# A mixture of experts in which the chosen tokens are fetched as rows from device memory and transposed, where products with selection matrices gathered them

## The reference, cut to what matters

```python
def expert_choice_ffn(h, w_router, w_gate, w_up, w_down):
    cap = CAPACITY_FACTOR * S // N_EXPERTS            # 64
    aff = jax.nn.softmax(h @ w_router, axis=-1)
    gates, idx = lax.top_k(aff.transpose(0, 2, 1), cap)
    xe = h[bidx, idx]                                  # the chosen tokens of each expert
    hg = jnp.einsum('becd,edf->becf', xe, w_gate)
    hu = jnp.einsum('becd,edf->becf', xe, w_up)
    y = jnp.einsum('becf,efd->becd', jax.nn.silu(hg) * hu, w_down)
    y = y * gates[..., None]
    return jnp.zeros_like(h).at[bidx, idx].add(y)
```

## Time and profile before

| what | value |
|---|---|
| runs | 2341.9 us median, 2340.33 to 2350.0 |
| the profiled execution | 2344.44 us, its span 2342.6 us |
| mean granted TensorE clock | 0.943 |
| PE busy, whole span | 2090.0 us (89%) |
| experts, from the first product of the first pair to the end of the span | 1862.65 to 2342.6 us |

### The profile page before, as it was taken

How to read it: one execution, slowest core, us unless ns; L and a number is a source line. 1 busy time by engine, 2 the same in 40 slices (tenths; PEclk the granted TensorE clock), 3 DMA queues, 4 the chain that set the end, 5 groups by cost and what they waited for, 6 DMA issues and landing times. The chain is left out here.

```text
span 2342.6 us, 31825 instructions
## 1 busy us (share of the span) xinstructions
PE 2090.0 (89%) x12889; PEld 1039.2 (44%) x12889; DVE 952.7 (41%) x1775; ACT 440.6 (19%) x877; POOL 238.7 (10%) x191
## 2 busy tenths in 40 slices
PE   7989898798998998979798977887889699999998
PEld 3553435543463343564443433455534444444442
DVE  1049678441116778743223542394321511111112
ACT  1010442121002144111222332321111200000000
POOL 0020410000011230000004540500000000000000
PEclk9989999899999999989899988898989799999999
DMA  4225110211214401120102101221045299999997
GB/s 157 68 106 197 46 39 30 70 40 55 98 49 171 162 10 39 36 101 27 57 18 72 37 27 41 68 73 38 11 148 209 120 392 420 421 420 420 421 420 305
DMA packets 63470, 330.03 MB, mean 141 GB/s; under 512 B 7280, under 2 KB 9840, under 8 KB 34928
## 3 DMA queue, kind: packets, MB, share of 16 engines
q1 hardware_dynamic: 63344, 328.27, 36.6%
HBM read 321.16 MB, written 6.29 MB: 140 GB/s over the span
## 5 line engine op out<-in xcount | busy, mean ns | idle before, releaser
L424 PE MATMUL ps<-store,side_ring 128*128 128x512 f32 x824 | 408.4, 625 | 17.2 <-DMA side_ring<-in_w_rwkv 6.6
L424 PEld LDWEIGHTS ps<-store,side_ring 128*128 128x128 f32 x824 | 146.2, 195 | 191.8 <-issue 168.6
L2561 PE MATMUL ps<-expert_ring,xe 128*64 128x512 f32 x1024 | 225.0, 597 | 3.6 <-DMA expert_ring<-in_w_expert 1.9
L337 PE MATMUL ps<-store,side_ring 128*128 128x512 f32 x384 | 169.5, 604 | 1.9 <-DVE store L303 1.9
L424 PE MATMUL ps<-store 128*128 128x512 f32 x256 | 122.9, 638 | 24.7 <-DMA store<-in_w_merge 24.1
L2561 PEld LDWEIGHTS ps<-expert_ring,xe 128*64 128x64 f32 x1024 | 73.3, 138 | 151.9 <-issue 149.8
L337 PEld LDWEIGHTS ps<-store,side_ring 128*128 128x128 f32 x384 | 74.5, 195 | 95.7 <-issue 93.4
L2589 PE MATMUL ps<-expert_ring,store 128*64 128x512 f32 x512 | 111.6, 594 | 1.4 <-DVE store L2646 1.4
L1641 PE MATMUL ps<-store,raw 128*128 128x512 f32 x256 | 110.7, 593 | 1.9 <-DVE store L303 1.9
L2618 ACT ACTIVATE store<-ps 128x1024 f32<-128x1024 f32 x16 | 16.4, 1024 | 420.5 <-PE ps L2561 420.5
L424 PEld LDWEIGHTS ps<-store 128*128 128x128 f32 x256 | 51.8, 205 | 93.4 <-issue 67.2
(11 more groups left out here) (430 smaller groups left out, 3148.7 us busy)
## 6 DMA issues: line engine op xcount, KB each, us to landing
expert_ring<-in_w_expert SPq DMA_DIRECT2D x192, 1024.0 KB, 16.8
mixed<-in_w_ada SPq DMA_DIRECT2D x24, 1024.0 KB, 4.8
side_ring<-in_w_attn SPq DMA_DIRECT2D x32, 512.0 KB, 3.7
side_ring<-in_w_rwkv SPq DMA_DIRECT2D x20, 512.0 KB, 4.2
raw<-in_ple_gate SPq DMA_DIRECT2D x16, 512.0 KB, 3.5
store<-in_w_merge SPq DMA_DIRECT2D x16, 512.0 KB, 3.9
side_ring<-in_w_conv SPq DMA_DIRECT2D x12, 512.0 KB, 3.3
gates_before<-gated SPq DMA_DIRECT2D x16, 256.0 KB, 2.0
```

What stands on the lines that cost most here:

```text
L337: last = nc.tensor.matmul(ps[:, u, :], ring[:, u, k, :], src[:, k, :], start=(k == 0), stop=(k == kt - 1))
L424: ins = self.nc.tensor.matmul(self.ps[:, self.banks[j % banks], :], self.ring[:, j % self.slots, k, :], self.src[:, k, :], start=(k == 0), ...
L2561: last = nc.tensor.matmul(ps[w, 2 * ep + half, :], xe[:, ep, k, :], ring[:, unit % SLOTS, k2, S * half:S * half + S], start=(k == 0), stop ...
```

## The change

The first pair is gathered as before. For the other seven pairs, the rows of `tokens` are written to a table in device memory (`token_rows`, 512 rows of 4 KB) by four transfers on SP's queue. 28 products with one column each (`number`) multiply `chosen` with a new constant, `token_number`, and give for each pair the list of 128 token numbers; DVE copies it to an integer tile. GpSimd then issues for each pair an indirect transfer that fetches 128 rows of 4 KB into one of two buffers, which lie over the first half of `tokens`. In the PE order of a pair, 4 transposes (`turn_rows`) stand in the place of each half of the gather. The loops over pairs now hold two pairs (`BODY = 2`), so that the two buffers have fixed addresses; SP's loop holds one turn of the ring. The order of the weights is the same.

```diff
+    parts["token_number"] = i[:, None] + P * np.arange(TT)[None, :]
...
-                with sp.Fori(0, PAIRS - 1) as r:
-                    for i in range(UNITS):
-                        j = i + SLOTS
-                        sp.wait_ge(used[i % SLOTS], r * TURNS + i // SLOTS + 1)
-                        sp.dma_start(ring[:, i % SLOTS], w_expert[r + j // UNITS, j % UNITS]).then_inc(landed[i % SLOTS], 16)
...
+                sp.wait_ge(h_copied, KT)
+                for t in range(TT):
+                    sp.dma_start(rows_out[t * P:(t + 1) * P, :], tokens[:, t, :]).then_inc(s["rows_out"], 16)
+                with sp.Fori(1, PAIRS * UNITS // SLOTS) as turn:
+                    for i in range(SLOTS):
+                        sp.wait_ge(used[i], turn)
+                        sp.dma_start(ring[:, i], w_expert[turn * SLOTS + i]).then_inc(landed[i], 16)
+                sp.wait_ge(s["rows_landed"], PAIRS - 1)
...
+                def number():
+
+                    for i in range(1, PAIRS):
+                        for t in range(TT):
+                            last = nc.tensor.matmul(ps[:, 3, i:i + 1], chosen[:, t, 2 * i:2 * i + 2, :].rearrange("p e c -> p (e c)"),
+                                                    M.c("token_number")[:, t:t + 1], start=(t == 0), stop=(t == TT - 1))
+                    last.then_inc(s["numbered"], 1)
+
+                def turn_rows(tiles, buf):
+
+                    for k in tiles:
+                        last = nc.tensor.transpose(ps[:, k // 4, (k % 4) * P:(k % 4 + 1) * P], rows[:, buf, k * P:(k + 1) * P],
+                                                   M.c("ident"))
+                        if k % 4 == 3:
+                            last.then_inc(s["gathered"], 1)
...
                         if not final:
-                            gather(range(4 * ep, 4 * ep + 4), lambda t: chosen[:, t, bass.ds(r * 2 + 2, 2), :].rearrange("p e c -> p (e c)"))
+                            if ep == 0:
+                                pe.wait_ge(s["rows_landed"], r + 1)
+                            turn_rows(range(4 * ep, 4 * ep + 4), (1 + half_body) % 2)
...
                 gather(range(KT), lambda t: chosen[:, t, 0:2, :].rearrange("p e c -> p (e c)"), 6)
                 pe.wait_ge(s["all_chosen"], TT)
-                pair(0, first=True)
-                with pe.Fori(1, PAIRS - 1) as r:
-                    pair(r)
-                pair(PAIRS - 1, final=True)
+                number()
+                pair(-1, 1, first=True)
+                with pe.Fori(0, PAIRS // BODY - 1) as b:
+                    for half_body in range(BODY):
+                        pair(b, half_body)
+                pair(PAIRS // BODY - 1, 0, final=True)
...
+            @block.gpsimd
+            def _(pool):
+                pool.wait_ge(s["numbers_ready"], 1)
+                pool.wait_ge(s["rows_out"], 16 * TT)
+                pool.wait_ge(s["gathered"], 2)
+                for i in range(1, PAIRS):
+                    if i >= 3:
+                        pool.wait_ge(s["gathered"], 2 * (i - 1))
+                    nc.gpsimd.indirect_dma_start(rows[:, (i - 1) % 2, :], None, rows_out,
+                                                 bass.IndirectOffsetOnAxis(ap=numbers[:, i:i + 1], axis=0)).then_inc(row[i - 1], 16)
+                    pool.wait_ge(row[i - 1], 16)
+                    pool.sem_inc(s["rows_landed"], 1)
...
                     nc.vector.tensor_copy(xe[:, :, 4 * b:4 * b + 4, :], gathered(6 + b)).then_inc(s["x_ready"], 1)
+                dve.wait_ge(s["numbered"], 1)
+                nc.vector.tensor_copy(numbers[:, 1:PAIRS], ps[:, 3, 1:PAIRS]).then_inc(s["numbers_ready"], 1)
```

More of the change, by code:

```diff
@@ L2456, with slot_of, turn_of @@
 PAIRS, UNITS, SLOTS = 8, 24, 12
-TURNS = UNITS // SLOTS
+BODY = 2
+TURNS = BODY * UNITS // SLOTS
+def slot_of(half, i):
+    return (UNITS * (1 + half) + i) % SLOTS
+def turn_of(b, half, i):
+    return b * TURNS + (UNITS * (1 + half) + i) // SLOTS
 def first_experts(nc, ring, w_expert, landed, busy, merge_taken, merge_done):
@@ L2469, in _, with experts @@
                     sp.wait_ge(merge_taken, KT)
-                sp.dma_start(ring[:, i], w_expert[0, i]).then_inc(landed[i], 16)
-def experts(nc, M, w_expert, tokens, chosen, aff, slot, extra, room, back, gain, x, out, ring, landed, h_copied, first_chosen):
+                sp.dma_start(ring[:, i], w_expert[i]).then_inc(landed[i], 16)
+def experts(nc, M, w_expert, rows_out, tokens, chosen, aff, slot, extra, room, back, gain, x, out, ring, landed, h_copied, first_chosen):
     ps = M.ps
@@ L2481, in experts @@
         sb = lambda name, shape: buffer(nc, stack, name, shape)
-        xe = sb("xe", [P, 2, KT, 64])
+        xe, rows = sb("xe", [P, 2, KT, 64]), tokens[:, 0:2, :]
+        numbers = stack.enter_context(nc.sbuf_tensor(f"numbers_{nc.next_id()}", [P, PAIRS], U32))
+        w_expert = w_expert.rearrange("r u p k n -> (r u) p k n")
+        row = [stack.enter_context(nc.semaphore(f"row_landed_{i}")) for i in range(1, PAIRS)]
         flat = lambda first, tiles: room[:, first:first + tiles, :].rearrange("p k n -> p (k n)")
@@ L2490, in experts @@
                    summed=0, added=0, gathered=0, all_chosen=0, weighted=0, back_turned=0, back_copied=0,
-                   stored=0) as (block, s):
+                   stored=0, rows_out=0, numbered=0, numbers_ready=0, rows_landed=0) as (block, s):
             used = s["used"]
@@ L2495, in _ @@
             def _(sp):
-                with sp.Fori(0, PAIRS - 1) as r:
-                    for i in range(UNITS):
-                        j = i + SLOTS
-                        sp.wait_ge(used[i % SLOTS], r * TURNS + i // SLOTS + 1)
-                        sp.dma_start(ring[:, i % SLOTS], w_expert[r + j // UNITS, j % UNITS]).then_inc(landed[i % SLOTS], 16)
-                for i in range(UNITS - SLOTS):
-                    sp.wait_ge(used[i % SLOTS], (PAIRS - 1) * TURNS + i // SLOTS + 1)
-                    sp.dma_start(ring[:, i % SLOTS], w_expert[PAIRS - 1, i + SLOTS]).then_inc(landed[i % SLOTS], 16)
+                sp.wait_ge(h_copied, KT)
[6 more added lines that the diff above has]
+                sp.wait_ge(s["rows_landed"], PAIRS - 1)
                 for m in range(KT):
@@ L2540, in scatter, with pair @@
                                          start=True, stop=True).then_inc(s["summed"], 1)
-                def pair(r, first=False, final=False):
+                def pair(b, half_body, first=False, final=False):
+                    r = b * BODY + (1 + half_body)
+                    slot = lambda unit: slot_of(half_body, unit)
                     def arrived(unit):
-                        pe.wait_ge(landed[unit % SLOTS], r * (16 * TURNS) + 16 * (unit // SLOTS) + 16)
+                        pe.wait_ge(landed[slot(unit)], turn_of(b, half_body, unit) * 16 + 16)
                     for ep in range(2):
@@ L2561, in pair @@
                                         last = nc.tensor.matmul(ps[w, 2 * ep + half, :], xe[:, ep, k, :],
-                                                                ring[:, unit % SLOTS, k2, S * half:S * half + S],
+                                                                ring[:, slot(unit), k2, S * half:S * half + S],
                                                                 start=(k == 0), stop=(k == KT - 1))
                                         if k2 == 1 and half == 1:
-                                            last.then_inc(used[unit % SLOTS], 1)
+                                            last.then_inc(used[slot(unit)], 1)
                     if not first:
@@ L2589, in pair @@
                                     last = nc.tensor.matmul(ps[w, 6 + half, :], act_t[:, ep, f, :],
-                                                            ring[:, units[ep] % SLOTS, f2, S * half:S * half + S],
+                                                            ring[:, slot(units[ep]), f2, S * half:S * half + S],
                                                             start=(f == 0), stop=(f == KT - 1))
                                     if f2 == 1 and half == 1:
-                                        last.then_inc(used[units[ep] % SLOTS], 1)
+                                        last.then_inc(used[slot(units[ep])], 1)
                 pe.wait_ge(h_copied, KT)
@@ L2613, in _, with silus @@
             def _(act):
-                def silus(r, first=False):
+                def silus(b, half_body, first=False):
+                    r = b * BODY + (1 + half_body)
                     for ep in range(2):
                         last = 8 * ep + 7
-                        act.wait_ge(used[last % SLOTS], r * TURNS + last // SLOTS + 1)
+                        act.wait_ge(used[slot_of(half_body, last)], turn_of(b, half_body, last) + 1)
                         nc.scalar.activation(act_in[:, ep, :], ps[:, 2 * ep:2 * ep + 2, :].rearrange("p b n -> p (b n)"),
@@ L2624, in silus @@
```

(22 more changed lines are left out.)

## The result

The changed kernel takes 2357.48 us (median of 8 runs, 2353.97 to 2360.75) against 2342.61 us before (8 runs): ratio 1.0061, 95% interval 1.0052 to 1.0070, or 14.9 us slower. Forecast were 2354 us and slower by more than 0.5% as the likeliest sign. The profiled execution took 2356.88 us, its span is 2355.1 us, 12.5 us over that of before.

What follows compares the result with a forecast made beforehand. The stream of weights at 420 GB/s was taken to bound the kernel; list + 6.3, fetches + 9.0, rests - 2.7 and first fetch - 0.6 gave + 12.0 us, so 2354 us (+ 0.51%), range 2345 to 2369 us.

Steps and rivals of the forecast that it cites:

- The weights set the end: Experts: weights take 59.92 us a pair at 420 GB/s, 1.55 us longer than PE; the last pair waits for their landing.
- PE saves 4.0 us a pair, worth nothing: Between second expert's and down products: 5.02 us in place of 9.03, 28 us in seven pairs, nothing directly off the end.
- A fetch costs its bytes, 1.28 us: Each indirect transfer of 0.524 MB takes the full engines 1.28 us, 9.0 us for seven; dearer fetches had chance 0.22.
- 9.0 - 0.6: Seven fetches cost 9.0 us, less 0.6 for half the first fetch running before the refill starts.
- The rests, - 2.7: Stretches after refilling starts where transfers were not full: early fetches and earlier first-pair down products fill 2.7 of 3.0 us.
- the 3.0: Transfer engines' rest in the earlier trace, from shares: 0.11 of 6 us and 0.23 of 10 us, 3.0 us in all.
- The second rest: The later stretch of transfers not full, 0.23 of 10 us; the first pair's down products come 2.7 us earlier against the refill.
- The list, 6.3 us: Before the first pair: 28 one-column products, 56 entries, take 6.3 us, unhidden, and delay the refill by as much.
- the lower clock only as a bound: The list in front of the first pair at the lower clock: 12.6 us, the upper bound beside the 6.3 taken.
- the forecast of 12.0: Sum of the terms at the end of the kernel: + 6.3 + 9.0 - 2.7 - 0.6 = + 12.0 us.
- The tail, unchanged: From the last pair's waited-for landing to the end of its down products: 44.6 us, left alone as that pair has no gather.
- the 1.8 us kept for that: Last pair's tail: up to 1.8 us kept for products slowed by a lower granted clock after transposes; expected cost nothing.

Runs made afterwards that it cites:

- gather_late: The kernel before, with only the gather for the second pair moved behind the first pair's down products: 2349.59 us, ratio 1.0026.
- transposes_only: The changed kernel without list, table and fetches, leaving row transposes and loops of two pairs: 2344.61 us, ratio 1.0006 to the kernel before.
- no_fetch: The changed kernel without its seven indirect transfers; transposes read rows that stay in the buffers: 2351.04 us, ratio 1.0027 to the kernel before.
- double_fetch: The changed kernel with every fetch issued a second time after the first has landed: 2367.87 us, ratio 1.0100 to the kernel before.
- list_only: The kernel before with only the list of token numbers added in front of the first pair, result unused: 2353.45 us, ratio 1.0041.
- list_spread: The changed kernel with the list cut in three, 4 of 28 products left in front: 2353.34 us, ratio 1.0036 to the kernel before.

## Why the prediction was right

**The weights set the end.** Shown. From first refill to landing every profile but gather_late's is 412.9 us plus 1.27 to 1.28 per fetch behind the refill, plus rests of up to 3.9 us, whatever PE saves or does besides. gather_late sets the limit: this holds as long as PE does not fall behind, and before it was near to that.

**PE saves 4.0 us a pair, worth nothing.** Right: 5.01 us in place of 9.03, and transposes_only is the same as before. Rows, table and waits on rows cost PE nothing seen; of the transfers only the weights are waited for, 28.6 us in all, from the third pair on as forecast, though 4.8 us a pair and not 7.

**A fetch costs its bytes, 1.28 us.** Right: 1.27 and 1.28. Seven less the first one, free ahead of the refill, make 7.6 us; forecast were 9.0 - 0.6. By the Trainium skill, "DMA: Bandwidth & Descriptors", section "Anatomy of one DMA — SWDGE (gpsimd) path", an estimate was 3.2 us a fetch; as time of full engines these runs do not agree with it. As time to landing it is too short here: the first fetch, with no weights beside it, landed 4.26 us after its instruction ended (3.56 in double_fetch), and in double_fetch, with the weights beside them, GpSimd waited 7.7 to 9.2 us for later ones.

**The rests, - 2.7.** Mis-sized, and right in part by luck. The way from refill to landing lost 416.8 - 412.9 = 3.9 us of rest: the 3.0 were read from the shares of the earlier trace rows, while their rates, 324 and 302 of 420 GB/s, make 4.2. The fetches are not needed for it, as no_fetch has no rest either. The second rest goes with the earlier down products. The first stands behind the second expert's products of 15.65 us at a lower clock; in the ten other profiles, list_only and gather_late among them, these took 13.95 to 14.00, so it went with the clock of that execution and not with the change.

**The list, 6.3 us.** The term that was mis-sized most. The mechanism was right: nothing hides it and the refill starts that much later. But it took 7.64 to 7.68 us, in other profiles 9.19 to 9.21, and the products behind it 15.62 to 15.75 for 13.88: 9.4 to 11.1 us. I had read its pace from products of four columns at a clock of 1.00 and kept the lower clock only as a bound. At 1.00 that pace holds (3.47 us for 32 entries in list_spread); the step that failed is that the clock would stay there. With 11.1, and the tail's 0.7 (below), the sum is 11.1 + 7.6 - 3.9 + 0.7 = 15.5; with 9.4, 13.8. The runs' 14.9 lie between. That the forecast of 12.0 came this close is partly luck: the list was 3.1 to 4.8 us too short in it, and fetches and rests together were 2.0 us too dear. The profiled execution was only 12.5 longer; 1.6 us of what is missing is its gather, which happened to take 8.72 us and not the 10.34 of before.

**The tail, unchanged.** To the end of the down products it is 44.6 us, as forecast. To the span's end it is 60.1 us against 59.4; the 0.7 come behind the last sum that DVE adds into `x`, the last piece of the chain. In four of the others the last pair's down products took 15.3 to 17.0 us for 14.0; the most, 3.0 us more, is above the 1.8 us kept for that.

## What to carry to other kernels

Work saved on an engine that waits for a stream was worth nothing here; what the replacement added to the stream, or put ahead of its start, counted in full. Look for the point at which a stream that never rests again begins: each microsecond put before it was a microsecond at the end, and a transfer in the rest ahead of it was free. Before moving work out of a gap, price it by what it will cost in the open, and ask how far behind the second path is.

## What was not expected of the hardware

A fully busy PE lost its clock: in the 28 products of one column with weights of 128 x 128 the granted clock went from 1.00 to 0.50, and with 128 columns the products kept 1.00 and were faster, 6.25 against 7.64 us. And the clock at the same place differs between executions: the first gather took 8.72 to 8.81 us in some profiles and 10.30 to 10.34 in others, the last down products 14.0 to 17.0. What decides this no run here shows.
